# A two-layer hybrid trunk in fp32 on one core: turned blocks of q and k copied by GpSimd, and another order of the last projection

## What is computed

```python
def moba_layer(x, norm_g, w_in, q_norm, k_norm, w_out):
    h = rms_norm(x, norm_g)
    q, k, v, z = jnp.split(h @ w_in, 4, axis=-1)
    q = rope(rms_norm(heads(q), q_norm))
    k = rope(rms_norm(heads(k), k_norm))
    v = heads(v)
    o = moba_attention(q, k, v).transpose(0, 2, 1, 3).reshape(B, S, D_INNER)
    return x + (o * jax.nn.silu(z)) @ w_out
```

## Time and profile before

| | |
|---|---|
| median of 3 runs | 426.38 us (426.24 to 426.8) |
| the profiled execution | 427.27 us, of which the span of the instructions is 425.3 us |
| mean granted TensorE clock | 0.992 of full |
| PE, DVE, ACT, POOL busy | 416.2, 292.3, 237.0, 31.9 us |

### The profile page before, as it was taken

How to read it: one execution, slowest core, us unless ns; L and a number is a source line. 1 busy time by engine, 2 the same in 40 slices (tenths; PEclk the granted TensorE clock), 3 DMA queues, 4 the chain that set the end, 5 groups by cost and what they waited for, 6 DMA issues and landing times.

```text
span 425.3 us, 5551 instructions
## 1 busy us (share of the span) xinstructions
PE 416.2 (98%) x2126; PEld 356.1 (84%) x2126; DVE 292.3 (69%) x373; ACT 237.0 (56%) x430; POOL 31.9 (8%) x45
## 2 busy tenths in 40 slices
PE   9999999999999999999999999999999999959997
PEld 8989898988888888888888888888888888848885
DVE  3879987779885545358934799358983699833532
ACT  5755453535454443469639785379846797443310
POOL 0175000000000000111001100011001010000000
PEclk9999999999999999999999999999999999988999
DMA  8996868453555747337694567794877927861002
GB/s 269 387 353 213 262 217 322 180 205 114 195 197 168 224 124 222 117 105 241 247 331 119 182 209 236 248 299 147 269 214 215 323 95 272 290 205 50 0 2 99
DMA packets 45945, 86.78 MB, mean 204 GB/s; under 512 B 2528, under 2 KB 8288, under 8 KB 45920
## 3 DMA queue, kind: packets, MB, share of 16 engines
q1 hardware_dynamic: 45200, 85.37, 60.4%
q10 hardware_dynamic: 720, 1.07, 0.8%
HBM read 79.61 MB, written 6.82 MB: 203 GB/s over the span
## 4 chain that ended last, share of the span: by engine, by line
PE 89%; DVE 6%; DMA 3%; SPq 0%; issue 0%; ACT 0%; DVEq 0%
PE acc L633 23%; PE acc L635 23%; PE acc L634 23%; PE acc L656 3%; PE acc L678 3%; PE acc L677 3%; PE acc L675 3%; DMA between<-uT 2%; DVE w_lo L848 2%; PE acc L697 1%; PE aux L688 1%; PE aux L772 1%; PE aux L779 1%; PE aux L771 1%; PE aux L790 1%; PE aux L791 1%
## 5 line engine op out<-in xcount | busy, mean ns | idle before, releaser
L848 DVE TENSOR_TENSOR w_lo<-raw,w_hi 128x2048 fp32r<-128x2048 f32 x65 | 147.9, 2285 | 45.2 <-ACT w_hi L384 45.2
L384 ACT ACTIVATE w_hi<-raw 128x2048 fp32r<-128x2048 f32 x64 | 122.0, 1914 | 43.9 <-PE acc L635 31.0
L633 PE MATMUL acc<-w_hi,hT_hi 128*128 128x512 f32 x320 | 126.9, 397 | 0.0
L635 PE MATMUL acc<-w_hi,hT_lo 128*128 128x512 f32 x320 | 124.8, 390 | 0.0
L634 PE MATMUL acc<-w_lo,hT_hi 128*128 128x512 f32 x320 | 124.6, 389 | 0.0
L635 PEld LDWEIGHTS acc<-w_hi,hT_lo 128*128 128x128 f32 x320 | 60.1, 188 | 12.9
L634 PEld LDWEIGHTS acc<-w_lo,hT_hi 128*128 128x128 f32 x320 | 60.2, 188 | 11.9
L633 PEld LDWEIGHTS acc<-w_hi,hT_hi 128*128 128x128 f32 x320 | 60.1, 188 | 11.7
L633 PE MATMUL acc<-w_hi,aT_hi 128*128 128x512 f32 x160 | 64.7, 404 | 4.9 <-DVE aT_lo L1067 4.9
L634 PE MATMUL acc<-w_lo,aT_hi 128*128 128x512 f32 x160 | 63.2, 395 | 0.0
L635 PE MATMUL acc<-w_hi,aT_lo 128*128 128x512 f32 x160 | 63.1, 395 | 0.0
(11 more groups left out here) (126 smaller groups left out, 452.1 us busy)
## 6 DMA issues: line engine op xcount, KB each, us to landing
raw<-in_w_in_dram SPq DMA_DIRECT2D x46, 1024.0 KB, 6.7
raw<-in_w_out_dram SPq DMA_DIRECT2D x16, 1024.0 KB, 5.3
raw<-in_w_pool_dram SPq DMA_DIRECT2D x4, 1024.0 KB, 5.4
between<-wide SPq DMA_DIRECT2D x8, 512.0 KB, 3.9
raw<-in_w_in_dram SPq DMA_DIRECT2D x8, 256.0 KB, 7.5
wide<-between SPq DMA_DIRECT2D x16, 128.0 KB, 2.8
qkT<-between SPq DMA_DIRECT2D x16, 128.0 KB, 2.9
between<-uT SPq DMA_DIRECT2D x3, 512.0 KB, 10.0
```

Source lines behind the costliest of these rows:

```text
L384: act.activation(w_hi[:, slot, :], raw[:, slot, :], ACT.Copy).then_inc(hi_made, 1)
L633: pe.matmul(a, shi, whi, start=first and k == 0, stop=False)
L635: ins = pe.matmul(a, slo, whi, start=False, stop=last and k == GK - 1)
L848: dve.tensor_tensor(w_lo[:, slot, :], raw[:, slot, :], w_hi[:, slot, :].bitcast(F32), ALU.subtract).then_inc(w_split, 1)
```

## The change

The blocks of q and k no longer go through DRAM. POOL copies them: 16 instructions for q and 16 for k in each group, each of 32 partitions by 256 elements, from any of the four quarters of the partitions to any other (`place_blocks`). The moves of q and k leave SP's order and `lay_q` leaves ACT's. The move of `y1` stays.

The copies stand on POOL in the order q's root, q's copies, k's root, k's copies. POOL waits for the end of q's copies before it makes k's root.

In the out-projection granules (1, 0) and (1, 1) now come before (0, 2). `y1_hi` and `y1_lo` of group 2 stand one granule later, and `y1_lo` there behind the weights' split.

```diff
-OUT1_ORDER = [(0, 0), (0, 1), (0, 2), (1, 0), (1, 1), (1, 2), (0, 3), (1, 3)]
+OUT1_ORDER = [(0, 0), (0, 1), (1, 0), (1, 1), (0, 2), (1, 2), (0, 3), (1, 3)]
...
-                    if j == 3:
-                        move_q(g)
-                    if j == 5:
-                        move_k(g)
...
+            def place_blocks(dst, blocks, made):
+
+                for a in range(P // Q):
+                    for b in range(P // Q):
+                        to = dst[b * Q:(b + 1) * Q].rearrange("p h (t a i) -> p a t h i", t=TT, i=Q)[:, a]
+                        at = blocks[a * Q:(a + 1) * Q, b * 2 * P:(b + 1) * 2 * P].rearrange("p (t h i) -> p t h i", t=TT,
+                                                                                            h=HPG)
+                        ins = pool.tensor_scalar(to, at, 1.0, 1.0, ALU.mult, ALU.mult)
+                ins.then_inc(made, 1)
...
             for g in range(GROUPS):
                 norms(g, 0)
+                pool.wait_ge(qk_blocked[0], g + 1)
+                pool.wait_ge(scores_ready, HPG * g)
+                pool.wait_ge(qk_scaled, g + 1)
+                place_blocks(qT, scratch[0].rearrange("p t n -> p (t n)"), qkT_made[0])
+                pool.wait_ge(qkT_made[0], g + 1)
                 norms(g, 1)
+                pool.wait_ge(qk_blocked[1], g + 1)
+                pool.wait_ge(k_rstd_made, g + 1)
+                place_blocks(kT, scratch[1].rearrange("p t n -> p (t n)"), qkT_made[1])
+                pool.wait_ge(qkT_made[1], g + 1)
...
-                        act.wait_ge(qkT_landed[which], MOVED * g)
+                        act.wait_ge(qkT_made[which], g)
...
                 w(6)
-                lay_q(g)
                 w(7)
...
-                if j == 1:
+                if j == 2:
                     y1_hi(last - 1)
...
-                pe.wait_ge(qT_made, TT * (g + 1))
-                pe.wait_ge(qkT_landed[1], MOVED * (g + 1))
+                pe.wait_ge(qkT_made[0], g + 1)
+                pe.wait_ge(qkT_made[1], g + 1)
...
-                if j == 1:
-                    y1_lo(last - 1)
...
+                if j == 2:
+                    y1_lo(last - 1)
```

More of the change, by code:

```diff
@@ L141, in bass_hybrid_trunk @@
         qT = qkT[:, 0]
-        kT = qkT[:, 1].rearrange("p h s -> p (h s)").rearrange("p (a t h i) -> p t h a i", a=P // Q, t=TT, h=HPG)
+        kT = qkT[:, 1]
         y1_blocks = uT[:, :, :].rearrange("p f s -> p (f s)")[:, 0:TT * COLS]
@@ L201, in bass_hybrid_trunk @@
         qk_blocked = [sem("q_blocked"), sem("k_blocked")]
-        qT_made = sem("qT_made")
-        qkT_landed = [sem("qT_landed"), sem("kT_landed")]
+        qkT_made = [sem("qT_made"), sem("kT_made")]
         y1_blocked, y1T_landed = sem("y1_blocked"), sem("y1T_landed")
-        qk_stored, y1_stored = [sem("q_stored"), sem("k_stored")], sem("y1_stored")
+        y1_stored = sem("y1_stored")
         scores_ready, bias_made, exp_made = sem("scores_ready"), sem("bias_made"), sem("exp_made")
@@ L209, in bass_hybrid_trunk @@
         dve_chain, pool_chain = sem("dve_chain"), sem("pool_chain")
-        between = [nc.dram_tensor(f"between{i}", (P, TT * COLS), F32, kind="Internal").ap() for i in range(3)]
+        between = [nc.dram_tensor(f"between{i}", (P, TT * COLS), F32, kind="Internal").ap() for i in range(1)]
         block = ctx.enter_context(nc.Block())
@@ L274, in flat @@
                 return buf.rearrange("p t n -> p (t n)")
[L276 to L283, removed]
             def move_y1(g):
                 sp.wait_ge(y1_blocked, g + 1)
-                move_blocks(y1_blocks, y1_blocks, between[2], g, y1_stored, y1T_landed)
+                move_blocks(y1_blocks, y1_blocks, between[0], g, y1_stored, y1T_landed)
             for i in range(8 * GROUPS + 8):
@@ L534, in tanh_z @@
                                    scale=rstd_half[:, t:t + 1]).then_inc(tanh_made, 1)
[L536 to L542, removed]
             def y1_hi(g):
@@ L770, in scores @@
                 s = aux[h % 2]
-                pe.matmul(s[:, 0:P], qT[:, h, 0:P], kT[:, 0, h], start=True, stop=True)
-                pe.matmul(s[:, P:3 * P], qT[:, h, P:SEQ], kT[:, :, h], start=True, stop=True).then_inc(scores_ready, 1)
+                pe.matmul(s[:, 0:P], qT[:, h, 0:P], kT[:, h, 0:P], start=True, stop=True)
+                pe.matmul(s[:, P:3 * P], qT[:, h, P:SEQ], kT[:, h, :], start=True, stop=True).then_inc(scores_ready, 1)
             def turn_probs(g, h):
```

## The result

The changed kernel takes 474.74 us (median of 4 runs, 472.11 to 476.08) against 426.59 us before. The ratio is 1.1118, with a 95% interval of 1.1062 to 1.1175. It is slower by 48 us where 33.9 were forecast: inside the range, 15 us above the 460 us of the forecast.

The account below looks back on a forecast made before the run. PE, busy 98% of the span, bounds the kernel through its waits and clock. Group delays of 8.2 + 9.0 + 10.1 + 11.5, plus 2.4 slow clock, less 7.3, give 33.9 us more: 460 us, range 438 to 494.

Parts of the forecast that it names:

- the 7.3 us: PE's 4.9 us wait for group 2's y1 in the out-projection and 2.4 us of slow clock behind it both go.
- The copy's price: One POOL copy of 256 elements a partition takes 0.41 us; one per 0.37 us, bounds 0.30 and 0.60.
- a pitch of 0.45: Case within the forecast of about 460: copies following each other every 0.45 us give about 474 us.
- Turns with DVE: POOL gets one instruction in behind each two-operand DVE instruction; DVE pays 0.25 us for each copy of 256 elements.
- Steps 1 and 2: Group 2: q's copies take 10.2 us, delaying k's root, scale_k, rotation and w(5)'s split; PE waits 5.5 us, then 2.4 slow.
- Step 3: k's copies in group 2, slowed beside DVE, end at 328.5; scores come 10.1 us late, PE's second wait is 2.2 us.
- the term for the clock: Behind PE's second waits at the scores, only the last group gets a slow stretch, 2.4 us.
- POOL holding the port over a whole burst (3): Rival, 8%: DVE waits 5.9 us in w(3) and in w(5); 7 us a group and its clock, some 455 us.
- "The copies fit" (4): Rival, 16%: no exclusion for 32-partition instructions; q's copies end at 301.5 and the kernel is faster, 421.8 us.
- "Copies dear" (2): Rival, 12%: short runs and other partitions make the pitch 0.60 us, 6.0 us a group more; 490 to 496 us.

Follow-up runs that it names:

- Experiment 1: The kernel before with only the new out-projection order and the later y1_hi and y1_lo, q and k still through DRAM: 419.94 us, ratio 0.9846.
- experiment 6: The changed kernel, but each copy goes to the same 32 partitions that it reads, so blocks stand in wrong places: 466.16 us in one run.
- experiment 7: The changed kernel with the copies' two loops exchanged, so four in a row write one quarter and read different ones: 475.86 us in one run.
- Experiment 8: The changed kernel with 8 instead of 16 copies for k in groups 1 to 3: 457.22 us, ratio 1.071.
- Experiment 4: The changed kernel with layer 1's splits w(3) to w(7) replaced by one-operand DVE turns of raw, low parts left out: 434.15 us, ratio 1.018.

## Why the prediction was right, and by how much it was off

**What bounds, and the 7.3 us: right.** Experiment 1 measured 6.6 us by its ratio and 7.5 by the spans.

**The copy's price.** 0.41 us was forecast and 0.40 is measured. The distance from one copy to the next was mis-sized: 0.46 us, not 0.37, because the quarter changes from each copy to the next (experiments 6 and 7). In group 2 it makes q's burst 11.2 instead of 10.2 us and k's 14.05 instead of 13.4. Experiment 6 gives it a price in the whole kernel: 474.7 - 466.2 = 8.6 us, from one run, where the runs of the changed kernel spread over 4 us. The prediction had about 474 for a pitch of 0.45. That this meets the measured time is partly luck: it allowed 14 us between the two pitches where experiment 6 shows 8.6, and at 0.37 it lacked 6 us.

**Turns with DVE: right.** q's burst has two copies of 2.34 us, behind w(3) and w(4), as counted. DVE pays at most 0.2 us for one (2.49 against 2.28 for w(4)), where I had taken 0.25; w(3), which starts before the first copy, pays nothing (2.25 in the earlier trace rows, and 2.25 at 322.43 in the changed kernel), and w(5) and w(6) together 0.2 (4.71 against 4.49).

**Steps 1 and 2: right.** scale_k had been forecast 11.0 us late. In times from the end of q's blocks it began 1.0 us after them and now begins 335.57 - 322.51 = 13.1 after (the blocks are turned at 321.26 + 1.25), so 12.1 late. The first wait was forecast at 5.5 us and was 6.35 in group 2; the difference is q's longer burst.

**Step 3: the mechanism was right; the burst and, above all, the term for the clock were mis-sized.** I had the second wait of group 2 at 2.2 us and gave only the last group a slow stretch behind it. With the longer bursts the second waits were 3.0 to 4.1 us and the clock fell behind each of them. The scores of the four groups came later than the group before made them by 11.0, 14.2, 13.6 and 15.1 us (228.91, 293.44, 357.38 and 421.47 against 217.72, 268.07, 318.42 and 367.40, less the 0.2 us by which this trace runs behind at the start of group 0), where 8.2, 9.0, 10.1 and 11.5 were forecast. That is 53.9 against 38.8, 15.1 us more, and group 1 has the largest share, 5.2.

The bursts of q and k of groups 0 and 1 (those of group 2 stand above, and those of group 3 are as long):

```profile
194.92 11.30 POOL L347 TENSOR_SCALAR qkT<-wide 32x256 f32<-32x256 f32 x16 [9.42 <-DVE wide L1022]
...
215.66 13.16 POOL L347 TENSOR_SCALAR qkT<-wide 32x256 f32<-32x256 f32 x16 [7.70 <-DVE wide L1022]
...
259.50 11.23 POOL L347 TENSOR_SCALAR qkT<-wide 32x256 f32<-32x256 f32 x16 [13.67 <-DVE wide L1022]
...
280.17 13.18 POOL L347 TENSOR_SCALAR qkT<-wide 32x256 f32<-32x256 f32 x16 [7.70 <-DVE wide L1022]
```

The forecast had 10.0 and 12.0 us in group 0, 10.2 and 12.3 in group 1 (13.4 less twice 0.56), 10.2 and 13.4 in groups 2 and 3. So the bursts were 2.5, 1.9, 1.7 and 1.7 us longer, 7.7 in all. The windows behind the scores of groups 0 to 2, columns as in the earlier trace rows:

```profile
228.91:238.00 9.09, 9.09 (x28) 7.36 (x29) 3.10 (x6) 1.78 (x5) 0.00 (x0) 0.66 0.32 93
293.44:302.00 8.56, 8.55 (x35) 7.12 (x36) 3.10 (x6) 2.47 (x6) 0.00 (x0) 0.82 0.63 180
357.38:366.00 8.62, 8.62 (x34) 7.05 (x35) 3.10 (x6) 2.40 (x6) 0.00 (x0) 0.80 0.73 213
```

That is 6.2, 3.1 and 3.4 us at half clock, and half of it lost: 3.1, 1.5 and 1.7, 6.3 us in all, for which the prediction had nothing. Each delays q in the next group, which is why group 0 misses least and group 1, behind the longest stretch, most. 1.1 us are not accounted for. Experiment 8 shows the clock's part by itself. With the last group's slow stretch, 2.4 us as forecast, and less the 7.3 us, 53.9 is the whole change of the span: 49.0 = 474.3 - 425.3.

**The rivals.** POOL holding the port over a whole burst (3) is refuted: splits and copies alternate. "The copies fit" (4) needed a DVE that doesn't stand in the way. Experiment 4 makes it so, with the root where the change has it, and takes 434 us where the rival was worked out at 421.8: the 0.09 us between copies and the clock made even that case slower than before. "Copies dear" (2) was right in its kind: the pitch was 0.09 us above the forecast's, where the rival had 0.23. Its short runs were not the reason, since the same runs go at 0.37 in experiment 6.

## To carry to other kernels

Before an idle engine is given work, look at what it already does that others wait for: here a root of 1.65 us behind 11 us of copies held up three engines, while moved ahead of them it costs nothing. Price an instruction on GpSimd by how many DVE instructions with two SBUF operands run beside it, not by its own duration alone: one copy got in behind each. And a transfer that hides completely brings nothing when it is made faster; the order of the last granules, one line, brought all there was.

## What the runs showed of the hardware

- GpSimd copies of 32 partitions by 256 elements start every 0.46 us where the read or the written quarter of the partitions changes from one to the next, and every 0.37 where both stay, at the same duration of 0.40 us.
- A 32x32 turn on DVE with one operand lets GpSimd work beside it (bursts of 7.3 us); a subtraction of two operands of the same duration doesn't (11.2). Beside it one copy gets through for each subtraction, 2.34 us long.
- Hundredths of a microsecond between the starts can decide whether a GpSimd instruction waits. POOL's negated root of q took 0.20 us before and 2.33 in the changed kernel's groups 1 to 3, where it starts 0.03 to 0.04 us after a split instead of 0.02 to 0.04 before one. Nobody waited for it. The order of the starts alone doesn't settle it: the copy of k at 351.51 starts 0.02 us before the split w(7) and takes 2.54 us.
- The clock fell to half behind three of PE's waits of 2.4 us, and neither behind the one of 1.25 nor behind one of 2.6 in experiment 8. So the length of the wait alone doesn't settle it.
